# Two feed-forward layers of a transformer stack, their products cut into quarters: seven products of quarters in place of eight

## The reference, cut to what matters

```python
D_FF = 2816        # SEQ = D_MODEL = 1024, DEPTH = 2

def _swiglu(xn, w_gate, w_up, w_down):
    g = jnp.einsum('bsd,df->bsf', xn, w_gate)
    up = jnp.einsum('bsd,df->bsf', xn, w_up)
    return jnp.einsum('bsf,fd->bsd', jax.nn.silu(g) * up, w_down)

x = x + _rmsnorm(h, post_mix_g[layer])
h = _swiglu(_rmsnorm(x, pre_ffn_g[layer]), ffn_w_gate[layer], ffn_w_up[layer], ffn_w_down[layer])
x = x + _rmsnorm(h, post_ffn_g[layer])
```

## Time and profile before

| | |
|---|---|
| median of three runs | 4581.38 us (4580.41 to 4581.43) |
| the profiled execution | 4578.38 us, its span 4576.6 us, mean granted TensorE clock 0.941 |
| TensorE busy | 92% of the span, 19570 matmuls recorded |
| VectorE, ScalarE, GpSimd busy | 44%, 27%, 20% |
| DMA over the span | 59 GB/s on average |

### The profile page before, as it was taken

How to read it: one execution, slowest core, us unless ns; L and a number is a source line. 1 busy time by engine, 2 the same in 40 slices (tenths; PEclk the granted TensorE clock), 3 DMA queues, 4 the chain that set the end, 5 groups by cost and what they waited for, 6 DMA issues and landing times.

```text
span 4576.6 us, 47983 instructions
## 1 busy us (share of the span) xinstructions
PE 4199.5 (92%) x19570; PEld 3304.2 (72%) x19570; DVE 2026.7 (44%) x2559; ACT 1216.1 (27%) x1557; POOL 935.7 (20%) x458
## 2 busy tenths in 40 slices
PE   7899799999889998899999977998999999899778
PEld 6457688888666666778888866886888888766556
DVE  6744512222454443442222267223665565365553
ACT  4333321111232233221111133212222222155311
POOL 1002122222112332122222211222111111121141
PEclk9999899999999999999999988998999998899788
DMA  2002111111110000111111112322111112131232
GB/s 100 19 14 78 33 46 51 46 51 46 51 56 19 24 19 28 74 39 49 49 49 50 47 68 72 105 92 100 44 55 59 51 56 94 56 107 56 83 142 88
DMA packets 76836, 270.89 MB, mean 59 GB/s; under 512 B 8772, under 2 KB 9416, under 8 KB 72648
## 3 DMA queue, kind: packets, MB, share of 16 engines
q1 hardware_dynamic: 76616, 267.82, 16.9%
HBM read 219.55 MB, written 48.23 MB: 59 GB/s over the span
## 4 chain that ended last, share of the span: by engine, by line
PE 78%; DVE 15%; ACT 3%; issue 1%; DMA 1%; POOL 1%; SPq 0%; DVEq 0%; POOLq 0%; ACTq 0%
PE ps L357 51%; PE ps L428 7%; PE ps L765 2%; PE ps L2189 2%; PE ps L2201 2%; PE ps L1513 2%; PE ps L2197 2%; PE ps L1505 1%; PE ps L3239 1%; PE ps L2242 1%; DVE x L548 1%; DVE ps L617 1%; DVE n L3256 1%; DMA gb<-g_keep 1%; DVE ysq L530 1%
## 5 line engine op out<-in xcount | busy, mean ns | idle before, releaser
L310 POOL TENSOR_TENSOR wlo<-wraw,whi 128x1024 fp32r<-128x1024 f32 x301 | 723.5, 2404 | 2984.3 <-ACT whi L302 2877.8
L357 PE MATMUL ps<-xhi,whi 128*128 128x512 f32 x3024 | 985.7, 408 | 82.8 <-DVE xlo L554 49.1
L357 PE MATMUL ps<-xlo,whi 128*128 128x512 f32 x3024 | 948.0, 395 | 0.0
L357 PE MATMUL ps<-xhi,wlo 128*128 128x512 f32 x3024 | 945.5, 394 | 0.0
L302 ACT ACTIVATE whi<-wraw 128x1024 fp32r<-128x1024 f32 x301 | 319.0, 1060 | 2056.8 <-PE ps L357 1727.6
L357 PEld LDWEIGHTS ps<-xhi,whi 128*128 128x128 f32 x3024 | 571.5, 192 | 235.1 <-issue 48.6
L617 DVE TENSOR_TENSOR ps<-ps,t 128x1024 f32<-128x1024 f32 x161 | 198.4, 1233 | 1083.8 <-PE ps L357 1069.2
L357 PEld LDWEIGHTS ps<-xlo,whi 128*128 128x128 f32 x3024 | 577.3, 191 | 124.1
L357 PEld LDWEIGHTS ps<-xhi,wlo 128*128 128x128 f32 x3024 | 577.3, 191 | 124.0
L428 PE MATMUL ps<-xhalf,whi 128*128 128x512 f32 x1024 | 379.8, 453 | 4.5 <-POOL wlo L310 4.5
L357 PE MATMUL ps<-xhalf,whi 128*128 128x512 f32 x1024 | 282.0, 398 | 26.6 <-DVE xhalf L554 13.4
(11 more groups left out here) (484 smaller groups left out, 4935.8 us busy)
## 6 DMA issues: line engine op xcount, KB each, us to landing
wraw<-in_w_dram SPq DMA_DIRECT2D x301, 512.0 KB, 3.5
g_keep<-gates SPq DMA_DIRECT2D x64, 256.0 KB, 2.4
gb<-g_keep SPq DMA_DIRECT2D x32, 512.0 KB, 5.1
p_keep<-stage SPq DMA_DIRECT2D x30, 512.0 KB, 2.9
x<-in_x_dram SPq DMA_DIRECT2D x8, 1024.0 KB, 9.8
x_keep<-x SPq DMA_DIRECT2D x8, 1024.0 KB, 3.8
x<-x_keep SPq DMA_DIRECT2D x4, 1024.0 KB, 7.8
n<-p_keep SPq DMA_DIRECT2D x8, 512.0 KB, 6.9
```

Source lines behind the costliest of these rows:

```text
L310: ge.own().tensor_tensor(K.lo(c), K.raw[:, c % NRAW, :], K.hi(c).bitcast(F32), SUB).then_inc(*K.G(("lo", c)))
L357: done = pe.e.matmul(into[:, h, :], wt, x[h], start=(first and j == 0), stop=(last and j == 2), skip_group_check=True)
```

## The change

Two of the 22 inner blocks are still made as before: their four tiles of gates and ups are 32 block products. The other 20 inner blocks, in twos, and the whole down product are done by quarters. A product of a 2 x 2 arrangement of weight quarters (two output row blocks by two parities of the inner row blocks) with a 2 x 2 arrangement of activation quarters (the two parities by the two halves of the tokens) is made of seven products of sums of quarters (Strassen's scheme in Winograd's form) instead of eight.

A **block** `b` of the new schedule is such a set of seven products, made for two things side by side (gate and up, or two pairs of output row blocks). Blocks 0 to 9 are gate and up, with 4 pairs of inner row blocks; each of their products is 2 x 4 x 3 = 24 matmuls (L1261). Blocks 10 to 17 are the down product in four groups (`GROUPS`: 2, 3, 3, 3 pairs), two blocks to a group, with 12 or 18 matmuls to a product. That is 2604 matmuls, with 192 in the four plain tiles 2796 for a layer.

What is added. VectorE makes four sums of weight quarters for each block (`weight_sum`), the sums of the activations' quarters, and the recombination of the seven products out of three pairs of banks `X`, `Y`, `Z` (`seven_vector`, `seven_finish`), on which products 3 to 6 pile up in place once ScalarE or VectorE has read the earlier one (`GUARD`). Each product has a weight operand of its own to split, so there are 126 splits in a layer where there were 62, besides those of the four plain chunks. The inner activations' seven quarters go to memory (`keep_h`, 256 KB each, 77 in a layer) and come back as the down product's operands before each group (`activation_load`, 28 in a layer), and are split then (`operand_high`, `operand_low`). The residual input goes to memory too and is loaded again in the last block.

```diff
-FG = [3, 3, 3, 3, 3, 3, 2, 2]
-NA = 4
...
+NB1 = 10
+GROUPS = [2, 3, 3, 3]
+NB = NB1 + 2 * len(GROUPS)
+PLACE = "XYZYXYZ"
+GUARD = {3: "U2", 4: "s1", 5: "U3", 6: "C22"}
+SLOT_OPERAND = (0, 4, 6, 2, 1, 3, 5)
+SUM_OF = {1: 2, 2: 1, 3: 3, 6: 4}
+RAW_OF = {0: 0, 4: 3, 5: 2}
...
+def pairs_of(b):
+    return 4 if b < NB1 else GROUPS[(b - NB1) // 2]
...
+def seven_tensor(pe, K, F, b):
+    n, k = F.name, pairs_of(b)
+    for j in range(7):
+        if j < 3:
+            take(pe, K, K.P, (n, PLACE[j]), b)
+        else:
+            pe.wait_ge(*K.at(n, GUARD[j], b))
+        out, hi, lo, c = F.psum(K, b, PLACE[j]), F.ohi[j], F.olo[j], 7 * b + j
+        if set_of(b) or j in (1, 2, 3, 5):
+            pe.wait_ge(*K.at(n, "op", set_of(b), j))
+        pe.wait_ge(*K.at(n, "wlo", c))
+        for s in range(2):
+            for i in range(k):
+                o = part(s * k + i)
+                for t, (w, x) in enumerate(((F.whi(c), hi), (F.whi(c), lo), (F.wlo(c), hi))):
+                    d = pe.e.matmul(out[:, s, :], w[:, o], x[:, i, :], start=(j < 3 and i == 0 and t == 0), stop=(i == k - 1 and t == 2), skip_group_check=True)
+        d.then_inc(*K.T((n, "p", b, j)))
...
+def seven_high(se, K, F, c):
+    n, (b, j) = F.name, divmod(c, 7)
+    se.wait_ge(*K.at(*F.source_event(b, j)))
+    if c >= 3:
+        se.wait_ge(*K.at(n, "p", *divmod(c - 3, 7)))
+    elif c:
+        se.wait_ge(*K.at("chunk", F.c0 + 1 + c))
+    se.own().activation(F.whi(c), F.source(b, j), ACT.Copy).then_inc(*K.S((n, "whi", c)))
...
+def operand_high(se, K, F, g, j):
+    k = GROUPS[g - 1]
+    se.wait_ge(*K.at(F.name, "hin", g, j))
+    se.own().activation(F.ohi[j][:, :k, :], F.olo32[j][:, :k, :], ACT.Copy).then_inc(*K.S((F.name, "ohi", g, j)))
...
+def weight_sum(ve, K, F, b, i):
+    n, V, w = F.name, K.V, 256 * pairs_of(b)
+    a = [F.raw(b, r) for r in range(4)]
+    s1, s2 = F.S1[:, :w], F.S2[:, :w]
+    if i == 1:
+        ve.wait_ge(*K.at(n, "raw", 4 * b + 1))
+        ve.wait_ge(*K.at(n, "raw", 4 * b + 2))
+        if b:
+            ve.wait_ge(*K.at(n, "wlo", 7 * b - 5))
+        ve.own().tensor_tensor(s1, a[1], a[2], ADD).then_inc(*V((n, "S", b, 1)))
+    elif i == 2:
+        ve.wait_ge(*K.at(n, "raw", 4 * b))
+        if b:
+            ve.wait_ge(*K.at(n, "wlo", 7 * b - 1))
+        ve.own().tensor_tensor(s2, s1, a[0], SUB).then_inc(*V((n, "S", b, 2)))
+    elif i == 3:
+        ve.own().tensor_tensor(a[1], a[1], a[0], SUB).then_inc(*V((n, "S", b, 3)))
+    else:
+        ve.wait_ge(*K.at(n, "raw", 4 * b + 3))
+        ve.wait_ge(*K.at(n, "wlo", 7 * b + 1))
+        ve.own().tensor_tensor(s2, a[3], s2, SUB).then_inc(*V((n, "S", b, 4)))
...
+def operand_low(ve, K, F, g, j, source=None):
+    k = 4 if g == 0 else GROUPS[g - 1]
+    source = F.olo32[j] if source is None else source
+    ve.wait_ge(*K.at(F.name, "ohi", g, j))
+    ve.own().tensor_tensor(F.olo[j][:, :k, :], source[:, :k, :], F.ohi[j][:, :k, :].bitcast(F32), SUB).then_inc(*K.V((F.name, "op", g, j)))
...
+def activation_product(ve, K, F, b, x):
+    n, t, p = F.name, F.buf(b, (2, 0, 3, 1)[x]), b + 1
+    ve.wait_ge(*K.at(n, "silu", b, x))
+    if p > 1:
+        ve.wait_ge(*K.at(n, "stored", p - 1, SLOT_OPERAND[x]))
+    ve.own().tensor_tensor(F.hq[x], t[:, 0, :], t[:, 1, :], MUL).then_inc(*K.V((n, "h", p, x)))
...
+def activation_sums(ve, K, F, p):
+    n, V, h = F.name, K.V, F.hs(p)
+    def before(slot):
+        if p > 1:
+            ve.wait_ge(*K.at(n, "stored", p - 1, SLOT_OPERAND[slot]))
+    ve.own().tensor_tensor(h[3], h[3], h[0], SUB).then_inc(*V((n, "h sum", p, 3)))
+    before(4)
+    ve.own().tensor_tensor(h[4], h[2], h[3], SUB).then_inc(*V((n, "h sum", p, 4)))
+    before(5)
+    ve.own().tensor_tensor(h[5], h[0], h[4], SUB).then_inc(*V((n, "h sum", p, 5)))
+    before(6)
+    ve.own().tensor_tensor(h[6], h[1], h[4], SUB).then_inc(*V((n, "h sum", p, 6)))
...
+def seven_finish(ve, K, F, b):
+    n, V = F.name, K.V
+    z = F.psum(K, b, "Z")
+    ve.wait_ge(*K.at(n, "p", b, 6))
+    u2 = F.buf(b, 1)
+    if b < NB1:
+        ve.own().tensor_tensor(u2, u2, z, ADD).then_inc(*V(F.free(b, "Z")))
+        ve.own().tensor_tensor(u2, u2, F.half_rows(1), MUL).then_inc(*V((n, "scaled", b, 3)))
+    else:
+        out = F.quarter(b, 3)
+        for s in range(2):
+            first = out[:, s, :] if set_of(b) > 1 else u2[:, s, :]
+            events = [(n, "done", b, 3, s), *([(n, "done", b, 3), F.free(b, "Z")] if s else [])]
+            ve.own().tensor_tensor(out[:, s, :], first, z[:, s, :], ADD).then_inc(*V(*events))
...
+def seven_vector(ve, K, F, b, j):
+    n, V = F.name, K.V
+    up, more = b < NB1, set_of(b) > 1
+    s1, u2, u3 = (F.buf(b, i) for i in range(3))
+    x, y, z = (F.psum(K, b, p) for p in "XYZ")
+    if j == 2:
+        ve.wait_ge(*K.at(n, "s1", b))
+        ve.wait_ge(*K.at(n, "p", b, 1))
+        ve.own().tensor_tensor(u2, s1, y, ADD).then_inc(*V((n, "U2", b)))
+        if more:
+            out = F.quarter(b, 3)
+            ve.own().tensor_tensor(out, out, u2, ADD).then_inc(*V())
+    elif j == 3:
+        weight_sum(ve, K, F, b, 4)
+    elif j == 4:
+        if b == NB1:
+            for i in range(7):
+                ve.wait_ge(*K.at(n, "stored", NB1, i))
+        ve.wait_ge(*K.at(n, "p", b, 3))
+        ve.own().tensor_tensor(u3, s1, y, ADD).then_inc(*V((n, "U3", b)))
+        ve.wait_ge(*K.at(n, "p", b, 2))
+        c22 = F.buf(b, 3) if up else F.quarter(b, 2)
+        ve.own().tensor_tensor(c22, c22 if more else u3, z, ADD).then_inc(*V((n, "C22", b), *([] if up or more else [(n, "done", b, 2, 0)])))
+        if b + 1 < NB:
+            weight_sum(ve, K, F, b + 1, 1)
+    elif j == 5:
+        if up:
+            ve.own().tensor_tensor(F.buf(b, 3), F.buf(b, 3), F.half_rows(1), MUL).then_inc(*V((n, "scaled", b, 2)))
+        elif more:
+            out = F.quarter(b, 2)
+            ve.own().tensor_tensor(out, out, u3, ADD).then_inc(*V((n, "done", b, 2, 0)))
+        ve.wait_ge(*K.at(n, "p", b, 4))
+        if up:
+            ve.own().tensor_tensor(u3, x, F.half_rows(0), MUL).then_inc(*V((n, "scaled", b, 0), F.free(b, "X")))
+        elif more:
+            out = F.quarter(b, 0)
+            ve.own().tensor_tensor(out, out, x, ADD).then_inc(*V((n, "done", b, 0, 0), F.free(b, "X")))
+            out = F.quarter(b, 1)
+            ve.own().tensor_tensor(out, out, s1, ADD).then_inc(*V())
+        else:
+            ve.own().tensor_copy(F.quarter(b, 0), x).then_inc(*V((n, "done", b, 0, 0), F.free(b, "X")))
+        if b + 1 < NB:
+            weight_sum(ve, K, F, b + 1, 2)
+    elif j == 6:
+        ve.wait_ge(*K.at(n, "p", b, 5))
+        if up:
+            ve.own().tensor_tensor(s1, s1, y, ADD).then_inc(*V(F.free(b, "Y")))
+            ve.own().tensor_tensor(s1, s1, F.half_rows(0), MUL).then_inc(*V((n, "scaled", b, 1)))
+            activation_product(ve, K, F, b, 2)
+            activation_product(ve, K, F, b, 0)
+        else:
+            out = F.quarter(b, 1)
+            ve.own().tensor_tensor(out, out if more else s1, y, ADD).then_inc(*V((n, "done", b, 1, 0), F.free(b, "Y")))
...
+def seven_low(ge, K, F, c):
+    b, j = divmod(c, 7)
+    ge.wait_ge(*K.at(F.name, "whi", c))
+    ge.own().tensor_tensor(F.wlo(c), F.source(b, j), F.whi(c).bitcast(F32), SUB).then_inc(*K.G((F.name, "wlo", c)))
...
+def activation_load(sy, K, F, g, j):
+    n, k, p = F.name, GROUPS[g - 1], first_pair(g)
+    sy.wait_ge(*K.at(n, "p", NB1 + 2 * (g - 1) - 1, j))
+    for i in range(p, p + k):
+        sy.wait_ge(*K.at(n, "stored", i, j))
+    sy.e.dma_start(F.olo32[j][:, :k, :], K.keep_h[j][:, p:p + k, :]).then_inc(*K.h_in[j]((n, "hin", g, j)))
...
-        self.F0 = Ffn(K, "f0", self.N1, gain("post_ffn_g0"))
+        self.F0 = Ffn(K, "f0", self.N1, gain("post_ffn_g0"), self.O0, 24, 0, 65)
-    ffn_sync(sy, K, S.F0, 24)
+    ffn_sync(sy, K, S.F0)
```

More of the change, by code:

```diff
@@ L1149, in ffn_tensor @@
 def ffn_tensor(pe, K, F):
[L1150 removed]
+    n = F.name
     pe.reach(n + " start")
[L1152 to L1163 removed]
@@ new lines, in squares_vector @@
+def squares_vector(ve, K, F, b, x, rows=(slice(0, 2),)):
+    n, acc, sq = F.name, F.ysq[:, HALVES[x in (2, 3)]], F.sq[x in (0, 3)]
+    for r in rows:
+        ve.wait_ge(*K.at(n, "squares", b, x, r.start))
+        if b == LASTS and x in (0, 2):
+            ve.own().tensor_tensor(acc, sq[:, 0, :], sq[:, 1, :], ADD).then_inc(*K.V((n, "squares added", b, x)))
+        else:
+            for s in range(r.start, r.stop):
+                ve.own().tensor_tensor(acc, acc, sq[:, s, :], ADD).then_inc(*K.V((n, "squares added", b, x), (n, "sum", int(x in (2, 3)))))
@@ L1203, in ffn_vector @@
 def ffn_vector(ve, K, F):
[L1204 removed]
+    n, X, V = F.name, F.X, K.V
     ve.fence(K, n + " start")
[L1206 to L1226 removed]
@@ L4062 @@
     arrays, at = layout(inp)
+    arrays["s"] = seven_stream(inp)
     lists = weight_stream(inp)
```

523 lines of the change are left out of this document (364 added, 159 removed).

## The result

The changed kernel takes **4558.0 us** (median of five, 4541.7 to 4559.5) against 4581.4 (4580.4 to 4586.8) for the kernel before: ratio 0.994, 95% interval 0.9922 to 0.9957. It is faster, by 23 us where 81 were forecast. The direction and the range held; the size did not.

What follows compares the result with a forecast made beforehand. TensorE's matmuls, 0.226 us each, were taken as the bound. Per layer 84.1 + 7.0 + 5.8 - 8 - 20.4 - 7.9 - 5.5 - 10 - 5 = 40.1 us, 80 for both: about 4500, range 4410 to 4560.

Steps and rivals of the forecast that it cites:

- The 84.1 us of matmuls: Feed-forward layers: 372 fewer matmuls a layer at 0.226 us each save 84.1 us a layer.
- The gains at the start and the end: Each layer's two ends: shorter TensorE waits, and less low clock at the start, save 7.0 and 5.8 us.
- The turns at the port: SBUF: VectorE instructions with two SBUF inputs alternate with GpSimd's splits, PSUM readers don't; without turns, layer-start waits are 5.7, not 20.4.
- The layer's start: First block of a layer: late operands, sums and splits make TensorE wait 20.4 us in all.
- Block 10: First down-product block: `U2` comes late behind the gates' remaining work, so TensorE waits 7.9 us.
- The gates' blocks: Gate-and-up blocks: TensorE waits some 0.9 us for `U2` in each of nine blocks, 8 us a layer.
- The clock ... 5 us: Three waits of 5 to 8 us a layer lower TensorE's clock, 1.6 to 3.4 each but not always: 5 us.
- I take the same price for the new ones.: New feed-forward products: each matmul costs 0.226 us, as before, so no added cost.
- The doubt that was named (one bank): New products: matmuls staying on one PSUM bank for 12 or so in a row might cost more than 0.226 us.
- the later down blocks: Down product after block 10: waits of 5.5 us in blocks 11 and 12, 10 us in two later pairs.
- 768 KB every 2.7 to 4.1 us ... some 4 us from issue, hidden: Down product: operand loads need up to 290 GB/s where 418 was seen, so they cost TensorE nothing.
- the loads are late: Rival: SyncE's queue order holds each of 28 loads a layer 1 us more, 4556; chance 0.11, shared with similar chains.

Runs made afterwards that it cites:

- The filler kernel: Against the changed kernel, TensorE makes 9 to 22 matmuls into an unused bank ahead of a layer's seven longest waits: 4542.2 us.

## Why the prediction was right in sign and wrong in size

**Held.** The 84.1 us of matmuls (84.3 in the account). The gains at the start and the end: the first gate's wait is gone, and the last wait ahead of the next norm's sums is 5.4 us where it was 7.6. The turns at the port: L1447's median of 2.70 us, L1521 always at 1.22. The waits below are idle time in the first layer. The layer's start: 15.9 us for 20.4, in the five places named, the last two 4.7 and 5.9 for 6.9 and 7.2. Block 10: 7.2 for 7.9. The gates' blocks: 3.2 us for 8, and 0.9 a block once the matmul was cheap, as counted.

**Failed: "The clock ... 5 us".** It measured 22.8 and 21.5 us a layer, 17.8 and 16.5 more than the 5 forecast. I had counted three waits of 5 to 8 us at 1.6 to 3.4 each. Eight places in the first layer lost 1.8 to 3.1 us each, 19 together: behind the long waits at 576, 596, 980, 1035, 1101 and 1171, behind 3.5 us at 1011, and behind a row of three short ones at 549 to 564. Fourteen more restarts cost some 0.24 to 0.29 each, 4 us, at full clock too: 0.16 is the busy time of the matmul ahead of the wait, and the rest is the second matmul behind it, which starts 0.31 to 0.34 us after the first in place of 0.227. The filler kernel shows that the time behind the long waits belongs to the waits.

**Failed: "I take the same price for the new ones."** 4 to 7 ns more in about two products of five, 9.4 us a layer, a term that the sum had at nothing. The doubt that was named (one bank) was refuted, and the cause is the place of the buffers in SBUF, weights against operand.

**Failed, in mechanism and in size: the later down blocks.** I put 5.5 and 10 us down to turns at the port (1.9 and 3.1 a pair). The waits were 8.0 in blocks 11 and 12 and 14.4 behind, 22.3 together for 15.5, and all but 6.2 went when the order alone was changed. They were the chain that the prediction called hidden, "768 KB every 2.7 to 4.1 us ... some 4 us from issue, hidden". The load was not slow (5.3 us to landing by the page); it was issued late, behind another load's wait on SyncE, and VectorE met it ahead of `U2`. That is the rival "the loads are late", in three or four places of a layer rather than 28, and its argument against itself (the product needs the load late) forgot that VectorE doesn't.

**Luck.** The idle time agrees with the forecast in the sum (+38.9 and +42.0 for +41.5) only since two misses cancel: the start and the gates' blocks were some 9 us shorter than forecast, the later down blocks 7 us longer. And that 4558.0 lies in the range is luck too: it is 2 us under the upper end, which was set there for late loads at every product, 4556, and not for a slow clock and a dearer matmul.

**Not foreseen.** The 5.3 us behind the second layer: at a layer's end the old program had issued the weight loads of the next stage five chunks ahead, the changed one issues three, and the kernel that loads two more has the loss back.
